# One decoder layer on one core: scale and key products moved to other engines, parameter loads and three steps placed elsewhere in the order

## The reference, cut to what matters

```python
def mixer_layer(x, h0, past_k, past_v, q_pos, k_pos, p):
    xn = rmsnorm(x, norm_g)
    u_a, z_a, q, k, v, z_b, g_a, g_b = jnp.split(xn @ w_in, SPLITS, axis=-1)
    y_a, h_last = s5_scan(u_a, h0, A_re, A_im, log_dt, B_re, B_im, C_re, C_im, D)
    y_a = jax.nn.gelu(y_a, approximate=False)
    y_a = y_a * jax.nn.sigmoid(y_a @ glu_w + glu_b)
    y_a = y_a * jax.nn.silu(z_a)
    o = sb_sweep(q, k_all, v_all, q_pos, k_pos, sb_bias) * jax.nn.silu(z_b)
    merged = jax.nn.sigmoid(g_a) * (y_a @ w_branch_a) + jax.nn.sigmoid(g_b) * (o @ w_branch_b)
    return x + merged @ w_out, k, v, h_last
# for 1024 prompt rows without a past, and for 8 new rows of 8 sequences with 256 past
# positions each, in two pages of 128; then y = rmsnorm(result, norm_f) for both.
```

## Time and profile before

| | us |
|---|---|
| median of three runs | 3028.0 |
| the profiled execution, its own time | 3026.5 |
| its span, from the first instruction to the last | 3024.7 |
| PE busy with matmuls | 2966.0 (98%) |
| DVE busy | 1345.2 (44%) |
| ACT busy | 1014.7 (34%) |
| POOL busy | 433.8 (14%) |

### The profile page before, as it was taken

One profiled execution on the slowest core, in us unless ns is written; L12 is line 12 of the kernel. 1 busy time (PEld: TensorE's weight loads), 2 busy tenths in 40 slices (PEclk: granted clock), 3 DMA queues, 4 the chain that ended last, 5 costly groups with the idle time before them and its releaser, 6 DMA issues.

```text
span 3024.7 us, 48779 instructions
## 1 busy us (share of the span) xinstructions
PE 2966.0 (98%) x19132; PEld 2904.7 (96%) x19132; DVE 1345.2 (44%) x2563; ACT 1014.7 (34%) x1210; POOL 433.8 (14%) x1118
## 2 busy tenths in 40 slices
PE   6999999999999999999999999999999999999998
PEld 5999999999999999999999999999999999999997
DVE  6624443452444345244434524443557544422266
ACT  5135215413521541362154135215421421221142
POOL 7400330240033023003302300320000000000000
PEclk8999999999999999999999999999999999999999
DMA  6332333233232223323322332332348754342283
GB/s 182 83 104 70 85 79 95 73 84 109 64 92 76 91 73 90 103 64 92 82 86 71 91 102 64 92 91 89 133 134 294 256 182 154 94 123 69 78 248 114
DMA packets 425730, 329.29 MB, mean 109 GB/s; under 512 B 64738, under 2 KB 387890, under 8 KB 423474
## 3 DMA queue, kind: packets, MB, share of 16 engines
q1 hardware_dynamic: 425522, 326.34, 36.0%
HBM read 235.72 MB, written 73.73 MB: 102 GB/s over the span
## 4 chain that ended last, share of the span: by engine, by line
PE 89%; POOL 3%; DVE 3%; issue 2%; ACT 1%; SPq 1%; DMA 1%; POOLq 0%; DVEq 0%; ACTq 0%
PE acc L1811 80%; PE side L1778 3%; PE side L1952 2%; PE side L1947 1%; POOL prologue L1164 1%; DVE work L1535 1%; ACT w_high L912 0%; PE side L1906 0%; PE side L1905 0%; PE side L2069 0%; DVE work L1542 0%; POOL prologue L1165 0%; POOL work L1266 0%; DMA work<-work 0%; SPq L509 0%
## 5 line engine op out<-in xcount | busy, mean ns | idle before, releaser
L1811 PE MATMUL acc<-x_high,w_high 128*128 128x344 f32 (+2 forms) x5440 | 1219.4, 327 | 10.6 <-ACT w_high L912 5.3
L1811 PE MATMUL acc<-x_low,w_high 128*128 128x344 f32 (+2 forms) x5440 | 1179.8, 320 | 0.0
L1811 PE MATMUL acc<-x_high,w_low 128*128 128x344 f32 (+2 forms) x5440 | 1176.1, 319 | 0.0
L1811 PEld LDWEIGHTS acc<-x_high,w_high 128*128 128x128 f32 x5440 | 907.7, 188 | 30.6 <-issue 14.2
L1811 PEld LDWEIGHTS acc<-x_low,w_high 128*128 128x128 f32 x5440 | 920.8, 189 | 0.0
L1811 PEld LDWEIGHTS acc<-x_high,w_low 128*128 128x128 f32 x5440 | 911.9, 188 | 0.0
L1380 DVE TENSOR_TENSOR w_low<-w_raw,w_high 128x1024 fp32r<-128x1024 f32 x233 | 287.6, 1234 | 602.8 <-ACT w_high L912 600.1
L912 ACT CAST w_high<-w_raw 128x1024 fp32r<-128x1024 f32 x232 | 242.3, 1044 | 889.5 <-PE acc L1811 806.3
L1257 POOL COPY work<-s_tables 128x28 f32 x16 | 3.3, 208 | 1505.7 <-DVE work L1528 1233.4
L1528 DVE TENSOR_TENSOR work<-work,side 128x128 f32<-128x128 f32 x64 | 18.4, 287 | 317.4 <-PE side L1952 317.4
L1778 PE MATMUL side<-work 128*128 128x128 f32 (+5 forms) x704 | 128.5, 310 | 1.7 <-POOL work L1276 1.7
(11 more groups left out here) (303 smaller groups left out, 2362.6 us busy)
## 6 DMA issues: line engine op xcount, KB each, us to landing
w_raw<-in_w_in SPq DMA_DIRECT2D x160, 512.0 KB, 3.9
w_raw<-in_w_out SPq DMA_DIRECT2D x48, 512.0 KB, 3.9
work<-t_sig_ga SPq DMA_DIRECT2D x24, 516.0 KB, 4.4
out<-work SPq DMA_DIRECT2D x18, 512.0 KB
t_qk<-stage SPq DMA_DIRECT2D x16, 516.0 KB, 5.0
work<-t_qk SPq DMA_DIRECT2D x16, 516.0 KB, 4.5
t_sig_gb<-stage SPq DMA_DIRECT2D x16, 516.0 KB, 4.3
t_sig_ga<-stage SPq DMA_DIRECT2D x16, 516.0 KB, 4.4
```

The lines of the kernel that those rows point to most:

```text
L1811: ins = mm(acc[s][:, a, 0:n], w[b][:, kk, :], x[:, kx, c0:c0 + n], start=start, stop=stop)
```

## The change

Seven edits are made together.

1. The parameters B and the state seeds of a turn's first half are loaded at the start of that turn, after the attention's output (`oz_sent`) has been stored; before, they were loaded near the end of the turn before. POOL's wait for `oz_ready` goes. The small buffers `pw`, `turn` and `u_new` lie behind the others instead of at the end of the work area.
2. KM of the first half stands at step 12 instead of 11.
3. In the prologue ACT scales the blocks 6 and 7 instead of DVE, and DVE takes the two copies of the start states instead of ACT.
4. The split of tile 6 of y stands at step 78 instead of 79.
5. The product with the cached keys is made by POOL instead of DVE.
6. PE waits for the last sigmoid of the GLU (`glu_n` at 8) before the first chunk of branch a, not before the second.
7. The sums of the new rows are made in one go at step 21 of the last 32 chunks instead of in three parts at steps 21 to 23; ACT's root moves from step 24 to 22 and DVE's use of it from step 25 to 23.

```diff
-    c.at = WORK - (12 * HG + 6 * HG + NEW)
@@ SP, phase_a
-                    sp.wait_ge(arg_ready, i * 8 + 8 + PRIMED)
-                    sp.wait_ge(ha_ready, i * 2 + 2)
-                    sp.wait_ge(kv_sent, i * 80 + 80 + PRIMED)
-                    load_s5(i * (2 * HG) + 2 * HG)
+                    sp.wait_ge(oz_sent, i * 16 + PRIMED)
+                    sp.wait_ge(kv_sent, i * 80 + PRIMED)
                 else:
                     sp.wait_ge(ha_ready, i * 2 + 1)
-                    load_s5(i * (2 * HG) + HG)
+                g0 = i * (2 * HG) + hf * HG
...
                 if cn == 0:
-                    sp.wait_ge(oz_sent, i * 16 + PRIMED)
+                    s5_params(0)
                     s5_seeds(0)
-                if cn == CHUNKS - 1 and not last:
-                    s5_params(0)
@@ tables of steps
-    TURN, BT, KM, PQ, ... = (4, 20), (8, 24), (11, 27), (13, 30), ...
+    TURN, BT, KM, PQ, ... = (4, 20), (8, 24), (12, 27), (13, 30), ...
-    Y_AT = (74, 74, 75, 76, 76, 77, 79, 79)
+    Y_AT = (74, 74, 75, 76, 76, 77, 78, 79)
@@ ACT, prologue
         x_high(3)
+        act.wait_ge(den_ready, 3)
+        for n in (6, 7):
+            nc.scalar.mul(x_block(n), x_block(n), nrstd[:, NEW + n:NEW + n + 1]).then_inc(x_scaled_a, 1)
...
-        act.wait_ge(par_mm, 3)
-        nc.scalar.mul(S_neg[0:64]..., acc[0][0:64, 0, :]..., -1.0)
-        nc.scalar.copy(S_in..., acc[0][:, 0, :]...).then_inc(s_seed_ready, 1)
-                if at == 24:
+                if at == 22:
                     act.wait_ge(var_ready, 6)
@@ POOL
-                if hf == 0:
-                    pool.wait_ge(oz_ready, 8 * i + PRIMED)
-                else:
+                if hf == 1:
                     pool.wait_ge(y_mm, 2 * i + 1)
...
+        for b in range(NEW):
+            pool.wait_ge(pg_k[b % 2], 32 * (b // 2 + 1))
+            pool.wait_ge(q_in[b % 2], 16 * (b // 2 + 1))
+            kb = kv[b % 2].rearrange("p (a n) -> p a n", a=N_PAGES)
+            nc.gpsimd.tensor_tensor(kb, kb, qbc[b % 2]..., ALU.mult).then_inc(kq_done, 1)
@@ DVE, prologue
-        for n in range(2):
-            x_low(2 + 2 * n)
-            x_low(3 + 2 * n)
-            scale(6 + n)
-        for n in range(6, KT):
+        V.tensor_copy(nnew[:, NEW + 6:NEW + 8], nrstd[:, NEW + 6:NEW + 8]).then_inc(den_ready, 1)
+        for n in range(2, KT):
             x_low(n)
         split_lo(0, 1)
         for n in range(KT, KT + 3):
             x_low(n)
+        dve.wait_ge(par_mm, 3)
+        V.tensor_scalar(S_neg[0:64]..., acc[0][0:64, 0, :]..., -1.0, None, ALU.mult)
+        V.tensor_copy(S_in..., acc[0][:, 0, :]...).then_inc(s_seed_ready, 1)
@@ DVE, branch a
-                dve.wait_ge(pg_k[n % 2], 32 * (n // 2 + 1))
-                dve.wait_ge(q_in[n % 2], 16 * (n // 2 + 1))
-                ch(V.tensor_tensor(kb, kb, qbc[n % 2]..., ALU.mult))
+                dve.wait_ge(kq_done, n + 1)
@@ DVE, last chunks
                 if at == 21:
-                    new_added()
-                if at == 22:
-                    new_sums(range(2))
+                    new_sums()
                 if at == 23:
-                    new_sums(range(2, 4))
-                    new_variance()
-                if at == 25:
                     n8 = newvar[0:NEW, :]
                     dve.wait_ge(std_ready, 6)
@@ PE
+        pe.wait_ge(glu_n, FT)
         for n in range(KT):
-            if n < 2:
-                pe.wait_ge(glu_n, FT - 1 + n)
-            else:
+            if n >= 2:
                 pe.wait_ge(br_a, n - 1)
```

More of the change, by code:

```diff
@@ L284, in build @@
     pre_mm, xs_sq, xs_hi = sem("prologue_mm"), sem("x_new_squares"), sem("x_new_high")
-    gcol_ready = sem("norm_g_col_ready")
+    gcol_ready, x_scaled_a = sem("norm_g_col_ready"), sem("x_scaled_by_act")
     squared, var_ready, std_ready, x_scaled_v, x_tr, x_hi, x_lo = [sem(s) for s in
@@ L309, in build @@
     pg_in, pg_k, pg_v, q_in = sem("pages_in"), [sem("page_k0"), sem("page_k1")], [sem("page_v0"), sem("page_v1")], [sem("q_in0"), sem("q_in1")]
-    zs_part, zs_tr, sarg_ready, sl_ready, sw_ready, sw_tr, swt_ready, spv_mm, ozs_ready = [sem(s) for s in
-        ("zs_part", "zs_tr", "sarg_ready", "slog_ready", "sw_ready", "sw_tr", "swt_ready",
+    kq_done, zs_part, zs_tr, sarg_ready, sl_ready, sw_ready, sw_tr, swt_ready, spv_mm, ozs_ready = [sem(s) for s in
+        ("kq_done", "zs_part", "zs_tr", "sarg_ready", "slog_ready", "sw_ready", "sw_tr", "swt_ready",
          "spv_mm", "ozs_ready")]
@@ L412, in load_y @@
             sp.dma_start(f32(XL[:, t, :]), t_y[t]).then_inc(tile_in[t], 16)
[L414 to L423, removed]
         def phase_a(i, last):
             if not last:
-                sp.lower_val(i * 80 + 80 + PRIMED)
                 for scale in (48, 64, 80, 128, 256, 512, 1024):
@@ L466, in s5_params @@
                 if hf == 0:
-                    sp.wait_ge(arg_ready, i * 8 + 8 + PRIMED)
-                    sp.wait_ge(ha_ready, i * 2 + 2)
-                    sp.wait_ge(kv_sent, i * 80 + 80 + PRIMED)
-                    load_s5(i * (2 * HG) + 2 * HG)
+                    sp.wait_ge(oz_sent, i * 16 + PRIMED)
+                    sp.wait_ge(kv_sent, i * 80 + PRIMED)
                 else:
                     sp.wait_ge(ha_ready, i * 2 + 1)
-                    load_s5(i * (2 * HG) + HG)
+                g0 = i * (2 * HG) + hf * HG
+                Bv = [x[0, bass.ds(g0, HG)].rearrange("g n c -> n g c") for x in (B_re, B_im)]
+                sp.dma_start(BcX[0:64], Bv[0]).then_inc(s5_in, 16)
+                sp.dma_start(BcX[64:128], Bv[1]).then_inc(s5_in, 16)
+                sp.dma_start(BmX[0:64], Bv[1]).then_inc(s5_in, 16)
+                sp.dma_start(BmX[64:128], Bv[0]).then_inc(s5_in, 16)
+                for f in range(2):
+                    sp.dma_start(h12[:, f], t_h[f][:, bass.ds(g0 * NEW, HG * NEW)].rearrange("p (g b) -> p g b", g=HG)).then_inc(s5_in, 16)
             def s5_seeds(hf):
@@ L807, in _ @@
         sp.wait_ge(st_sent, FT * 320 + PRIMED)
-    TURN, BT, KM, PQ, SCAN, ROT, YM, YS = (4, 20), (8, 24), (11, 27), (13, 30), (15, 32), (17, 34), (18, 36), (19, 37)
+    TURN, BT, KM, PQ, SCAN, ROT, YM, YS = (4, 20), (8, 24), (12, 27), (13, 30), (15, 32), (17, 34), (18, 36), (19, 37)
     YN, YT = 38, 40
@@ L1433, in _ @@
             x_low(n)
+        dve.wait_ge(par_mm, 3)
+        V.tensor_scalar(S_neg[0:64].rearrange("p (g b) -> p g b", b=NEW), acc[0][0:64, 0, :].rearrange("p (b g) -> p g b", b=NEW), -1.0, None, ALU.mult)
+        V.tensor_copy(S_in.rearrange("p (g b) -> p g b", b=NEW), acc[0][:, 0, :].rearrange("p (b g) -> p g b", b=NEW)).then_inc(s_seed_ready, 1)
         for n in range(KT + 3, 2 * KT):
@@ L1692, in weigh, with new_sums @@
             c2(V.tensor_tensor(hs, hs, nf[:, f, :].unsqueeze(1).broadcast_to([P, B2, P]), ALU.mult))
-        def new_added():
+        def new_sums():
             dve.wait_ge(osm_tr, 1)
@@ L1699, in new_added @@
                                    acc[s][0:NEW, 1:3, :].rearrange("p a (f n) -> p (a f) n", f=4), ALU.add))
-        def new_sums(quarters):
-            for q in quarters:
+            for q in range(4):
                 sq = stage[q % 2][0:NEW, 768:768 + 2 * P].rearrange("p (f n) -> p f n", f=2)
@@ L1707, in new_sums @@
                     c2(V.tensor_reduce(newsum[0:NEW, 2 * q + e:2 * q + e + 1], sq, axis=AX.XY, op=ALU.add))
-        def new_variance():
             n8 = newvar[0:NEW, :]
@@ L1800, in x_transposes @@
             for b in range(4):
-                if k == 0:
+                if k == 0 and 4 * half + b < 6:
                     pe.wait_ge(x_scaled_v, 4 * half + b + 1)
+                elif k == 0:
+                    pe.wait_ge(x_scaled_a, b - 1)
                 last = tr(x_bank(n)[:, b * P:(b + 1) * P], x_block(4 * half + b)[:, k, :], ident[:, :])
```

5 lines of the change are left out of this document (1 added, 4 removed).

## The result

The changed kernel took 3057.72 us (median of 3 runs, 3056.51 to 3058.63) against 3027.98: a ratio of 1.0104, with a 95% interval of 1.009 to 1.0117. The profiled span went from 3024.7 to 3056.1 us, 31.4 longer. All 20 executions of the changed kernel, later ones included, lie between 3056.5 and 3063.7. I had forecast 3040, made of the profiled execution and 12.9, rounded up. The sign was right, the size was not, and the time lies outside my range of 3031 to 3050.

What follows compares the result with a forecast made beforehand. PE was taken as the bound, busy 2966.0 of 3024.7 us. Terms 2.4 + 4.4 + 0 + 1.0 + 1.3 + 2.1 + 1.7 = 12.9 on the profiled 3026.5 gave 3039.4, predicted as 3040, range 3031 to 3050.

Steps and rivals of the forecast that it cites:

- KM one step later: First half of turns: chain from KM to v_ready moves 2.85 later, PE waits at YM; +4.4 us, bounds 0 and 22.8.
- rival B: Turns' first halves: POOL is late after the moved parameter loads, M comes 2 us late in seven turns; 3054 us, chance 15%.
- The waits at YM: Turns 1 to 7, first halves: PE waits 0.52 in turn 1, 1.23 in turn 7, 0.3 to 0.55 between; 3.8 us.
- Prologue: Before PE's first product: scalings on ACT and state copies on DVE delay it, 49.15 instead of 46.69; +2.4 us.
- Edit 1: Parameter loads of the first half: POOL starts 8.8 us later, covered by a reserve of 11.7; cost 0, bounds 0 and 8.
- Tile 6: Last turn, before PE's last PV: one cast of y stands before ACT's copy of transposed weights; +1.0 us.
- keys: GLU: POOL's key products stop DVE's two-input work, so PE waits for a low part; +2.1 us, bounds 0 and 6.8.
- sigmoid: Start of branch a: PE waits for the last sigmoid and a semaphore; +1.3 us, bounds 1.1 and 1.5.
- sums: Chunk 24 near the end: DVE's sums of the new rows delay the weights' split, PE waits; +1.7 us, bounds 0.8 and 3.
- C: Prologue and turn 0: relieved DVE wins 2.5, 0.50 and 1.90 us, so the kernel is faster; 3021.6 us, chance 3%.
- D: GLU: no exclusion where POOL comes first, so only the 2.1 us goes; 3038 us, counted as part of A.
- A: Prologue, GLU and YM: chains have more give, terms 0, 0 and 2.2 instead of 2.4, 2.1 and 4.4; 3033 us, chance 17%.

Runs made afterwards that it cites:

- the run with five equal waits: Kernel before, with DVE held back by chained memsets ahead of seven splits of branch b (eight memsets in five chunks, seven in two): span 3047.3 us.

## Why the prediction was wrong

**KM one step later: the step that failed.** I forecast 4.4 and it costs 20.9 (3056.1 less 3035.2). "It moves with KM by one step" was right; what I left out is who stands behind the moved instructions in a queue. SP issues in order, and the swaps are waits in SP's program. I had weighed the second half only against edit 1 (rival B: "the rows of the other half show no wait at BT"), and never asked what moves it, though its reserve at KM, 0.7, was the smallest of all. I priced the queue behind the loads of edit 1, not the queue behind the swaps. 12.4 of the miss of 18.5 are this, 1.6 of clock in turn 7 included. By the medians edit 2 costs 17.6 to 19.0, so its size is known to some 3 us; that it is four to five times my 4.4 is not in doubt.

**The waits at YM** are there, released by line 1502, in turns 1 to 6: 0.70 to 0.99 where I had 0.52 and 0.4. In turns 1 to 6 DVE goes on 3.5 to 3.8 us after the first swap's issue, where it was 2.9 to 3.1, and that adds to each. Turn 7, forecast at 1.23, shows no wait: there this stretch is as before, and the row for the Toeplitz transfers is 0.7 shorter (5.19 for 5.87). Size off by 1.75, mechanism as forecast.

**The clock** had no term: each wait was taken at its own length. It cost 3.1 in turn 0 and 1.6 in turn 7. The second belongs to edit 2. For the first this is not shown: the run with five equal waits is the kernel before up to there, and it too waits long at YM of turn 0 (3.26) and sees a fall.

**Prologue.** The instructions stand where I put them: the scalings from 33.16 (I had 32.1, and the last root ended 1.0 later in this run), the twelve low parts in 7.99, the first product 17.34 after the start of the root's last instruction, for which I had 17.4:

```profile
33.16 3.90 ACT L858 ACTIVATE rows_over_x_low<-rows_over_x_low,prologue 128x2048 f32<-128x2048 f32 x2 [0.82 <-DVE prologue L1418]
...
37.67 7.99 DVE L1388 SCALAR_TENSOR_TENSOR x_low<-acc,norm_g_col,x_high 128x512 fp32r<-128x512 f32 x12 [3.23 <-ACT x_high L830]
```

But the term passed to the end only in my sum. "Behind it PE, ACT and DVE go piece by piece as before" overlooks that PE waits 3 to 6 us in turn 0 anyway, for low parts, YM and the second KM, which take up a late start; alone the edit costs nothing by its medians. Edit 1, which I had at nothing, costs some 3 us by its medians. Its delay was right: in turn 2 POOL's first half starts 17.7 ahead of BT (603.35 and 621.00), before 26.4 (585.50 and 611.89), so 8.7 later where I had 8.8, and PE does not wait at BT.

**Tile 6, keys, sigmoid, sums** came within 0.5 of the forecast. The rows that answer: ACT's copy behind the cast and PE's 0.91 behind it; 1.21 for the sigmoid; 1.87 at chunk 24.

```profile
2190.68 1.00 ACT L956 COPY work<-side 128x1024 f32<-128x1024 f32 x1
2191.73 2.05 PE L1935 MATMUL side<-work 128*128 128x128 f32 x16 [0.91 <-ACT work L956]
...
2287.90 0.75 PE L1794 MATMUL acc<-x_high,w_high 128*128 128x344 f32 x3 [1.21 <-ACT stage L981]
...
3005.86 0.41 PE L1794 MATMUL acc<-x_high,w_high 128*128 128x384 f32 x1 [1.87 <-ACT w_high L1069]
```

At chunk 24 PE waits for ACT and not for DVE: ACT's second cast stands behind the root that waits for the sums (DVE ends them at 3004.5), and the split behind that cast. My 1.7 left ACT out.

**Rivals.** B had the right size (3054) and the right engine, POOL, for another reason and at another place. C and D did not happen; of A only the 0 for the prologue holds, in the medians of edit 3 alone, and not by DVE's total work but because turn 0 takes up the late start.

## What to carry to other kernels

When a step moves by one place, list for each queue what stands behind each instruction that moves with it, DMA issues above all, and look for the smallest reserve among those, in the other half of the loop too. A delay in front of a stretch in which the bound engine waits anyway is absorbed there; one inside a steady turn is paid in every turn. A new wait of 2 to 3 us of PE can cost more than its length, through the clock: 2.14 us cost another 1.5 here in some cases, 3.35 us another 3.1.

## What the runs showed of the hardware

The granted clock after a wait is not a function of the wait's length: 3.44 us were followed by full clock in turn 0 of the kernel with its loads between the swaps and by half clock in turn 0 of the kernel with edit 2 alone, 2.14 us by half clock three times in five, 2.01 us at one and the same place by half clock in seven kernels of thirteen, and a wait of 2.32 at one and the same place in turn 7 by half clock in three kernels of twelve. The falls seen lasted 3 to 7 us. And a POOL product that runs first holds a DVE instruction with two inputs in SBUF until it is done: 4.3 us, of a product of 5.05 us that began 0.6 before it.
